# A two-layer decoder trunk on one core: gate products of two blocks in six banks, and expert stages that end by column halves and row tiles

## The chip, the cores and the metric

The kernel runs on one core of a Trainium2 chip. The core has a matrix engine (TensorE, PE in the profile; its weight loads are PEld), VectorE (DVE), ScalarE (ACT), GpSimd (POOL) and SyncE (SP, which here only issues DMAs). Products land in PSUM, eight banks of 128 partitions by 512 fp32. The metric is the device time of one execution in microseconds, the median of the runs shown.

## The reference, cut to what matters

Two layers, 512 tokens of width 1024. Layer 0 mixes tokens with a gated linear recurrence (768 channels in four blocks of 192), layer 1 with sparse attention. After each mixer comes an output projection, and after that 32 gated experts of which each token uses two.

```python
xs, gate, xq = jnp.split(hn @ w_in, [LRU_WIDTH, 2 * LRU_WIDTH], axis=-1)
xs = causal_depthwise_conv(xs, conv_w, conv_b)
# rglru: xb is xs in 4 blocks of 192 channels
r = sigmoid(einsum('bsni,nij->bsnj', xb, w_a) + b_a)
i = sigmoid(einsum('bsni,nij->bsnj', xb, w_x) + b_x)
log_a = -8 * r * softplus(-lam);  a = exp(log_a)
u = sqrt(-expm1(2 * log_a)) * (i * xf);  h = scan(a, u)
y = h * gelu(gate)
...
x = x + mixed @ w_out[i]
x = x + hier_moe(rms_norm(x, norm_ffn[i]), ...)   # (silu(xb @ w_gate[e]) * (xb @ w_up[e])) @ w_down[e]
```

## The kernel before, in words

All five engines run their own instruction stream; semaphores order them. `plan()` numbers every product group ("job") of the part outside the expert stages; job n uses PSUM bank n mod 8, and `open_bank` makes TensorE wait until the job eight numbers earlier has been read. `filled` counts finished jobs. The order of jobs is written out by hand; `lru_order()` gives it for the recurrence.

**The recurrence of layer 0.** The 768 channels are six chunks of 128, feature-major: a chunk is 128 partitions by 512 tokens. For a chunk c there are four pieces of work: `conv` (TensorE projects the chunk, eight fp32 products, each of two records; ACT copies it out at L845; DVE convolves it at L1552 and L1556), `rec` (`block_gates(c)` makes the two gate products on TensorE at L1145; ACT and DVE then run the recurrence, L856 to L866 and L1566 to L1578), and `gate` (a projection and a gelu at L873). A block has 192 channels, so three chunks hold two blocks: the weights of chunk 0 are 128 rows deep and 64 rows deep in two terms, chunk 1 is made of two column halves with two terms each, chunk 2 is chunk 0 mirrored. Before, each `block_gates(c)` makes its own chunk: 4, 8 and 4 products for the three chunks of a pair of blocks, between projections. `xc_ready` counts chunks convolved.

**An expert stage.** Each layer has 16 pairs of experts. SP streams six 2 MB weight tiles for each pair into a ring of nine buffers (`pair_weights`, L503 and L506); the first are issued when `out.0.0` of the layer is filled. For a pair TensorE makes gate and up products (L1359), transposes the hidden rows (L1365) and the next tokens (L1352), makes the down product y in two column halves of 512 (L1373; `y_psum` counts the halves), and `combine` (L1381) adds y back to the token rows through a one-hot matrix: y is split into three bf16 parts, so each of four row tiles t needs 2 x 3 products. The split goes through ACT (L1011, L1014) and DVE (L1899, L1902). DVE adds a row tile of 1024 columns to x at L1906 (`c_psum`, `c_added`). The combine of pair n is made during pair n+1. That of the last pair stands behind the loop, after the whole split, in four banks, two row tiles at a time.

**The ends.** After the last adds of a layer DVE signals `moe_done` (L1955). In layer 1 ACT waits for it before `row_norm` (L770 square, L771 root), DVE normalises the rows (L1480), TensorE transposes them (L1064) and starts the projections of layer 1 (`project_two`, L1118). After the second layer SP waits for `moe_done` and issues the four output DMAs.

Of the kernel before, what the change touches and what calls it, by code (L numbers as in the profile page):

```python
# [23 lines left out]
ALU = mybir.AluOpType  # L24
# [3 lines left out]
P = 128  # L28
D = 1024
# [222 lines left out]
def hybrid_trunk(nc, a, out):  # L252
# [8 lines left out]
    with ExitStack() as ctx:  # L261
# [3 lines left out]
        def sem(name):  # L265
            return ctx.enter_context(nc.semaphore(name))
# [93 lines left out]
        xn_ffn = area(6 * UNIT, NT, D)  # L360

# [78 lines left out]
        stored = sem("stored")  # L440
# [51 lines left out]
        BANK_HT, BANK_XT = 0, (1, 4)  # L492

# [4 lines left out]
        def _(sp):  # L498
# [22 lines left out]
            for L in range(2):  # L521
# [78 lines left out]
                if L == 0:  # L600

                    sp.wait_ge(m["y_psum"], 2 * (NP - 1))
                    w = a["dsa_w_in"][0].rearrange("(p k) n -> p k n", k=KD)
                    sp.dma_start(w_in[1][:, :, 0:C_WI], w[:, :, 0:C_WI]).then_inc(ld["win"], 16)
                    sp.dma_start(w_in[1][:, :, C_WI:], w[:, :, C_XQ:]).then_inc(ld["win"], 16)
                n_ov = sp.value_load(ov_n[0:1, 0:1], min_val=0, max_val=OVMAX)
                with sp.If(n_ov > 0):
                    sp.wait_ge(scattered, 16 * 2 * NT * (L + 1))
                    sp.wait_ge(m["y_psum"], 2 * NP * (L + 1))
                    with sp.Fori(0, n_ov) as i:  # L610
                        e = sp.value_load(ov_list[0:1, bass.ds(i * 2, 1)], min_val=0, max_val=NE - 1)
# [7 lines left out]
                        wait_alone(sp, o["y_psum"], i * 2 + 2)  # L619
            sp.wait_ge(scattered, 16 * 2 * NT * 2)  # L620
# [115 lines left out]
        def _(act):  # L736
# [64 lines left out]
            for L in range(2):  # L801
# [12 lines left out]
                row_norm(L, "mix", NT, lambda t: x[:, t, :], lambda t: xn[:, t, :], x_ready)  # L814
# [201 lines left out]
                def pair(n, first=False):  # L1016
# [4 lines left out]
                    split(m, n)  # L1021

                pair(NP * L, first=L == 0)
                with act.Fori(1, NP) as i:
                    pair(i + NP * L)
                o = ov[L]
                act.wait_ge(ld["ovl"], 16 * (L + 1))
                n_ov = act.value_load(ov_n[0:1, 0:1], min_val=0, max_val=OVMAX)
                with act.If(n_ov > 0):
                    act.wait_ge(m["c_psum"], NT * NP * (L + 1))  # L1030
                    with act.Fori(0, n_ov) as i:
                        silu_of(o, i, slice(0, CAP))
                        hidden_out(o, i)
                        split(o, i, slice(0, CAP))


        @block.tensor
        def _(pe):
# [35 lines left out]
            for L in range(2):  # L1074
# [47 lines left out]
                if L == 0:  # L1122
                    def block_gates(c):

                        if c == 0:
                            pe.wait_ge(ld["wg"], 16 * 16)
                        pair, r = c // 3, c % 3
                        for g, nm in ((0, "ra"), (1, "rx")):
                            w = gate_w[:, g, pair]
                            x0, x1, x2 = (xc[:, 3 * pair + q, :] for q in range(3))  # L1130
                            pe.wait_ge(xc_ready, 3 * pair + (2 if r == 0 else 3))
                            b = open_bank(f"0.{nm}.{c}")
                            if r == 0:
                                todo = [(slice(0, P), 0, slice(0, P))]
                            elif r == 1:
                                todo = [(slice(0, 64), 0, slice(P, LB)), (slice(64, P), 1, slice(0, 64))]
                            else:
                                todo = [(slice(0, P), 1, slice(64, LB))]
                            for part, odd, cols in todo:
                                if odd == 0:  # L1140
                                    terms = [(w[:, 0, cols], x0), (w[0:64, 1, cols], x1[0:64])]
                                else:
                                    terms = [(w[64:P, 1, cols], x1[64:P]), (w[:, 2, cols], x2)]
                                for i, (l, rr) in enumerate(terms):
                                    ins = pe.matmul(b[part, :], l, rr, start=i == 0, stop=i == 1)  # L1145
                            ins.then_inc(filled, 1)

                    for what, c in lru_order():
                        if what == "rec":
                            block_gates(c)  # L1150
# [287 lines left out]
                combine_of(n0 + NP - 1, (0, 1, 2, 3))  # L1438
# [4 lines left out]
                with pe.If(n_ov > 0):  # L1443
                    pe.wait_ge(m["c_added"], NT * (n0 + NP))
# [20 lines left out]
                pe.wait_ge(moe_done, L + 1)  # L1465
# [3 lines left out]
        def _(dve):  # L1469
# [33 lines left out]
            for L in range(2):  # L1503
# [411 lines left out]
                def pair(n, p, first=False, second=False):  # L1915
# [12 lines left out]
                    split(m, n)  # L1928
# [12 lines left out]
                dve.wait_ge(m["c_added"], NT * (n0 + NP))  # L1941
                with dve.If(n_ov > 0):
                    with dve.Fori(0, n_ov) as i:
# [11 lines left out]
                dve.memset(small[:, 252:253], 0.0).then_inc(moe_done, 1)  # L1955
# [22 lines left out]
```

## Time and profile before

| | us |
|---|---|
| median of 3 runs (1555.86 to 1560.49) | 1558.89 |
| profiled execution, its own time | 1562.51 |
| its span | 1560.6 |
| TensorE busy | 1428.0 |
| VectorE busy | 599.3 |
| ScalarE busy | 332.1 |
| mean granted TensorE clock, share of full | 0.96 |

The span is the stretch of the profiled execution from its first to its last instruction; 1.9 us of its time lie around it. Busy shares are averages over stages with different limits, so the chain of waits and the timeline have to be read stage by stage.

### The profile page before, as it was taken

What the parts mean: (1) busy time and instruction counts of PE and PEld (TensorE: products, weight loads), DVE (VectorE), ACT (ScalarE), POOL (GpSimd) and SP (SyncE); (2) the same over time, 40 slices, a digit from 0 to 9 for tenths busy, and PEclk for the clock granted to TensorE, in tenths of its full rate; (3) what the DMA queues carried; (4) which work ended last, traced back from release to release, by engine and by line L of the source; (5) the groups of instructions that cost most, each with busy time, mean ns of one, the idle gap of its engine ahead of it and who ended that gap; (6) DMA issues with size and microseconds to landing.
All of it is one profiled execution on the core that took longest, in us unless ns stands there. A gap on an engine that the chain in (4) does not pass through costs nothing.

```text
span 1560.6 us, 16585 instructions
## 1 busy us (share of the span) xinstructions
PE 1428.0 (92%) x6233; PEld 627.5 (40%) x6233; DVE 599.3 (38%) x1094; ACT 332.1 (21%) x620; POOL 103.3 (7%) x199
## 2 busy tenths in 40 slices
PE   5999889599999989999799979995999999899997
PEld 4433545433333333333364545453333333333332
DVE  2563212423343332333349965124333433322333
ACT  3266311011111110111126755110111111110110
POOL 1000100110000000000000123002000000000000
PEclk9999999599999999999999989995999999999998
DMA  8700144499999999999720020544999999999993
GB/s 314 237 0 0 54 193 198 185 379 427 425 426 427 428 427 427 430 426 428 302 92 1 21 92 1 206 171 176 406 426 427 426 428 428 427 428 426 428 428 151
DMA packets 56249, 457.36 MB, mean 293 GB/s; under 512 B 15468, under 2 KB 20124, under 8 KB 31240
## 3 DMA queue, kind: packets, MB, share of 16 engines
q1 hardware_dynamic: 49108, 447.81, 69.4%
q0 software_dynamic: 5504, 8.68, 1.5%
q8 instruction: 33, 0.54, 0.1%
q10 hardware_dynamic: 1588, 0.20, 0.1%
q14 instruction: 16, 0.13, 0.0%
HBM read 459.50 MB, written 10.53 MB: 301 GB/s over the span
## 4 chain that ended last, share of the span: by engine, by line
PE 71%; DMA 21%; DVE 3%; ACT 2%; issue 1%; ACTq 1%; POOL 0%; DVEq 0%; SPq 0%; POOLq 0%
PE ps L1055 22%; PE ps L1359 20%; DMA arena<-in_moe_w_gate 14%; PE ps L1373 10%; PE ps L1381 7%; DMA arena<-in_moe_w_up 6%; PE ps L1305 2%; PE ps L1145 2%; PE ps L1352 2%; PE ps L1064 1%; PE ps L1244 1%; PE ps L1285 1%; PE ps L1365 1%; DMA mix<-scratch_xn,idx 0%; PE ps L1342 0%
## 5 line engine op out<-in xcount | busy, mean ns | idle before, releaser
L1359 PE MATMUL ps<-arena,xT 128*64 128x512 f32 x2048 | 461.7, 604 | 33.3 <-DMA arena<-in_moe_w_gate 27.3
L1359 PEld LDWEIGHTS ps<-arena,xT 128*64 128x64 f32 x2048 | 149.0, 139 | 329.5 <-issue 325.5
L1906 DVE TENSOR_TENSOR x<-ps,x 128x1024 f32<-128x1024 f32 x128 | 156.2, 1224 | 231.7 <-PE ps L1381 229.1
L1373 PE MATMUL ps<-arena,xT 128*64 128x512 f32 x1024 | 226.8, 595 | 0.0
L1381 PE MATMUL ps<-mix,xT 128*128 128x512 bf16 x768 | 179.7, 384 | 5.7 <-ACT mix L1014 5.7
L1055 PE MATMUL ps<-xT,arena 128*128 128x512 f32 x384 | 168.7, 595 | 1.1 <-issue 1.1
L1381 PEld LDWEIGHTS ps<-mix,xT 128*128 128x128 bf16 x768 | 70.6, 99 | 134.7 <-issue 52.6
L1373 PEld LDWEIGHTS ps<-arena,xT 128*64 128x64 f32 x1024 | 70.7, 137 | 131.8 <-issue 127.9
L1055 PE MATMUL ps<-arena,mix 128*128 128x512 f32 x256 | 112.7, 600 | 3.3 <-DMA arena<-in_w_out 2.6
L1055 PEld LDWEIGHTS ps<-xT,arena 128*128 128x128 f32 x384 | 72.0, 190 | 94.2 <-issue 92.6
L1899 DVE TENSOR_TENSOR mix<-ps,mix 128x512 f32<-128x512 f32 x64 | 44.3, 691 | 169.0 <-ACT mix L1011 169.0
L1889 DVE SCALAR_TENSOR_TENSOR xT<-ps,cur,xT 128x512 f32<-128x512 f32 x32 | 24.0, 751 | 209.1 <-PE ps L1359 209.1
L1005 ACT ACTIVATE xT<-ps 128x512 f32<-128x512 f32 x32 | 19.1, 597 | 387.5 <-PE ps L1365 387.5
L1011 ACT ACTIVATE mix<-ps 128x512 bf16<-128x512 f32 x64 | 38.2, 597 | 215.4 <-PE ps L1373 215.4
L1055 PEld LDWEIGHTS ps<-arena,mix 128*128 128x128 f32 x256 | 48.7, 192 | 63.3 <-issue 60.4
L675 POOL CAST idx<-tabP 128x1 int32 (+1 forms) x34 | 6.3, 186 | 971.4 <-PE ps L1352 779.2
L1001 ACT ACTIVATE xT<-ps 128x512 f32<-128x512 f32 x32 | 19.1, 597 | 234.6 <-PE ps L1359 234.6
L668 POOL TENSOR_SCALAR arena<-arena,small 128x256 f32<-128x256 f32 (+3 forms) x80 | 39.5, 514 | 303.9 <-DVE small L1629 236.8
L1883 DVE TENSOR_TENSOR xT<-ps,gains 128x512 f32<-128x512 f32 x68 | 43.8, 686 | 13.5 <-PE ps L1352 9.2
L1352 PE MATMUL ps<-ident,mix 128*128 128x128 f32 x272 | 37.8, 284 | 11.0 <-DMA mix<-scratch_xn,idx 11.0
L1759 DVE TENSOR_TENSOR x<-ps,x 128x512 f32<-128x512 f32 x16 | 11.1, 692 | 89.0 <-PE ps L1055 89.0
L1902 DVE TENSOR_TENSOR mix<-mix 128x512 bf16<-128x512 f32 x64 | 43.9, 687 | 3.1
(230 smaller groups left out, 1131.1 us busy)
## 6 DMA issues: line engine op xcount, KB each, us to landing
arena<-in_moe_w_gate SPq DMA_DIRECT2D x64, 2048.0 KB, 29.8
arena<-in_moe_w_up SPq DMA_DIRECT2D x64, 2048.0 KB, 31.1
arena<-in_moe_w_down SPq DMA_DIRECT2D x64, 2048.0 KB, 31.8
arena<-in_lru_w_in SPq DMA_DIRECT2D x2, 3072.0 KB, 16.5
arena<-in_dsa_w_in SPq DMA_DIRECT2D x1, 5120.0 KB, 15.6
arena<-in_w_mem_kv SPq DMA_DIRECT2D x2, 2048.0 KB, 9.0
scratch_xn<-arena SPq DMA_DIRECT2D x8, 512.0 KB, 8.0
arena<-in_w_out SPq DMA_DIRECT2D x1, 4096.0 KB, 13.6
```

Source lines behind the costliest of these rows:

```text
L668: ins = pool.tensor_scalar(buf[:, h, 0:width], buf[:, h, 0:width], inv[:, h:h + 1], 1.0, ALU.mult, ALU.mult)
L1011: act.activation(y_hi[part, c, :], ps[part, BANK_Y + c, :], ACT.Copy).then_inc(q["y_high"], 1)
L1055: ins = pe.matmul(b[part, cols], l, r, start=i == 0, stop=i == len(pairs) - 1)
L1145: ins = pe.matmul(b[part, :], l, rr, start=i == 0, stop=i == 1)
L1352: ins = pe.transpose(ps[:, BANK_XT[k // 4], (k % 4) * P:(k % 4) * P + n], xg[0:n, k::KD][:, 0:P], ident[0:n, 0:n])
L1359: ins = pe.matmul(ps[e * CAP:(e + 1) * CAP, bank, :], tokT[:, k, e * CAP:(e + 1) * CAP], rows_in[u][:, k, :], start=k == 0, stop=k == KD - 1)
L1373: ins = pe.matmul(ps[e * CAP:(e + 1) * CAP, BANK_Y + c, :], hT[:, j, e * CAP:(e + 1) * CAP], rows_down[u][:, j, c * 512:(c + 1) * 512], st ...
L1381: ins = pe.matmul(ps[:, 4 + 2 * (t % 2) + c, :], onehot[part, t * P:(t + 1) * P], y[part, c, :], start=q == 0, stop=q == 2)
L1883: dve.tensor_tensor(tokT[:, 4 * q:4 * q + 4, :], ps[:, BANK_XT[q], :].rearrange("p (k n) -> p k n", k=4), gains[:, 3 * L + 2, 4 * q:4 * q ...
L1899: dve.tensor_tensor(y_rest[part, c, :], ps[part, BANK_Y + c, :], y_hi[part, c, :], ALU.subtract).then_inc(q["y_rest"], 1)
L1902: dve.tensor_tensor(y_lo[part, c, :], y_rest[part, c, :], y_mi[part, c, :], ALU.subtract).then_inc(q["y_low"], 1)
L1906: dve.tensor_tensor(x[:, t, :], ps[:, b:b + 2, :].rearrange("p a n -> p (a n)"), x[:, t, :], ALU.add).then_inc(s_, 1)
```

## The change

Four edits. (1) `lru_order()` groups the recurrence: three `conv`, three `rec`, three `conv`, two `gate`, three `rec`, four `gate`. (2) `block_gates` is called once for a pair of blocks, opens six banks, waits for three convolved chunks, and issues its 16 products sorted by their shape: whole products, then the 64-row ones (upper and lower rows in turn), then the 64-column ones, the 64 by 64 ones, and whole ones again. (3) The last pair of each expert stage leaves the loops: its split is finished one column half at a time, its combine is made by column half over all eight banks (`last_bank`), and DVE adds 128x512 pieces (`half_added` counts the left ones, `c_added` the right ones). (4) In layer 1 `row_norm` of tile t waits for the two adds of its tile alone, writes its squares to a spare area (`rows_junk`), and a Sqrt of one column is issued ahead of it; and the output DMA of tile t is issued once the two adds of its tile are there, ahead of the overflow code (no expert block overflows with these inputs; no line of that code is in the profile).

```diff
 def lru_order():
-    steps = [("conv", c) for c in range(3)]
-    for c in range(NC):
-        steps += [("rec", c), ("conv", c + 3) if c < 3 else ("gate", c - 3)]
-    return steps + [("gate", c) for c in range(NC - 3, NC)]
+    steps = [("conv", c) for c in range(3)] + [("rec", c) for c in range(3)] + [("conv", c) for c in range(3, NC)]
+    steps += [("gate", 0), ("gate", 1)] + [("rec", c) for c in range(3, NC)]
+    return steps + [("gate", c) for c in range(2, NC)]
...
+        def last_bank(t, c):
+            return (jobs.number[f"1.xT.{t}.0"] + c) % 8
...
+                else:
+                    for t in range(NT):
+                        sp.wait_ge(half_added, NT * L + t + 1)
+                        sp.wait_ge(m["c_added"], NT * (2 * NP - 1) + t + 1)
+                        sp.dma_start(out[0, t * P:(t + 1) * P, :], x[:, t, :]).then_inc(stored, 16)
...
             sp.wait_ge(moe_done, 2)
-            for t in range(NT):
-                sp.dma_start(out[0, t * P:(t + 1) * P, :], x[:, t, :]).then_inc(stored, 16)
             sp.wait_ge(stored, 16 * NT)
...
                 def x_ready(t):
-                    if t == 0:
+                    if L:
+                        act.wait_ge(half_added, NT * (L - 1) + t + 1)
+                        act.wait_ge(m["c_added"], NT * (NP * L - 1) + t + 1)
+                    elif t == 0:
                         act.wait_ge(ld["x"], 16)
                 if L:
-                    act.wait_ge(moe_done, L)
+                    act.activation(small[:, 254:255], eps[:, 0:1], ACT.Sqrt)
...
+                def split_by_half(q, n):
+                    for c in range(2):
+                        act.wait_ge(q["y_psum"], n * 2 + (1 + c))
+                        act.activation(y_hi[:, c, :], ps[:, BANK_Y + c, :], ACT.Copy).then_inc(q["y_high"], 1)
+                        act.wait_ge(q["y_rest"], n * 2 + (1 + c))
+                        act.activation(y_mi[:, c, :], y_rest[:, c, :], ACT.Copy).then_inc(q["y_mid"], 1)
...
-                    def block_gates(c):
+                    def block_gates(pair):
+                        pe.wait_ge(xc_ready, 3 * pair + 3)
+                        x0, x1, x2 = (xc[:, 3 * pair + q, :] for q in range(3))
+                        bs = [[open_bank(f"0.{nm}.{3 * pair + r}") for nm in ("ra", "rx")] for r in range(3)]
+                        for g in gates:
+                            pe.matmul(bs[0][g], w[g][:, 0, 0:P], x0, start=True, stop=False)
+                        for g in gates:
+                            pe.matmul(bs[0][g], w[g][lo, 1, 0:P], x1[lo], start=False, stop=True).then_inc(filled, 1)
+                            pe.matmul(bs[2][g], w[g][hi, 1, 64:LB], x1[hi], start=True, stop=False)
+                        for g in gates:
+                            pe.matmul(bs[1][g][lo, :], w[g][:, 0, P:LB], x0, start=True, stop=False)
+                            pe.matmul(bs[1][g][hi, :], w[g][:, 2, 0:64], x2, start=True, stop=False)
+                        for g in gates:
+                            pe.matmul(bs[1][g][lo, :], w[g][lo, 1, P:LB], x1[lo], start=False, stop=True)
+                            pe.matmul(bs[1][g][hi, :], w[g][hi, 1, 0:64], x1[hi], start=False, stop=True).then_inc(filled, 1)
+                        for g in gates:
+                            pe.matmul(bs[2][g], w[g][:, 2, 64:LB], x2, start=False, stop=True).then_inc(filled, 1)
...
-                combine_of(n0 + NP - 1, (0, 1, 2, 3))
+                last = n0 + NP - 1
+                pe.wait_ge(m["c_added"], last * NT)
+                pe.wait_ge(m["xt_sbuf"], 2 * (NP + 1) * (L + 1))
+                pe.wait_ge(m["g_done"], last + 1)
+                for c in range(2):
+                    pe.wait_ge(m["y_mid"], last * 2 + (1 + c))
+                    pe.wait_ge(m["y_low"], last * 2 + (1 + c))
+                    for t in range(NT):
+                        for q, y in enumerate(y_parts):
+                            ins = pe.matmul(ps[:, last_bank(t, c), :], onehot[:, t * P:(t + 1) * P], y[:, c, :],
+                                            start=q == 0, stop=q == 2)
+                        ins.then_inc((half_psum, m["c_psum"])[c], 1)
...
-                pe.wait_ge(moe_done, L + 1)
...
+                def last_split(n):        # DVE; rest, low: one column half of L1899, L1902
+                    dve.wait_ge(m["c_added"], n * NT)
+                    rest(0)
+                    low(0)
+                    rest(1)
+                    add(0, 0)
+                    low(1)
+                    for t in range(1, NT):
+                        add(t, 0)
+                    for t in range(NT):
+                        add(t, 1)
...
-                with dve.Fori(2, NP) as p:
+                with dve.Fori(2, NP - 1) as p:
                     pair(p + n0, p)
-                add_of(n0 + NP - 1, range(NT))
+                pair(n0 + NP - 1, NP - 1, last=True)
```

## Rows read from the trace of the kernel before

**Rows 1.** Page: busy time of the engines; the last chain by engine.

```profile
PE 1428.0 (92%) x6233; PEld 627.5 (40%) x6233; DVE 599.3 (38%) x1094; ACT 332.1 (21%) x620; POOL 103.3 (7%) x199
...
PE 71%; DMA 21%; DVE 3%; ACT 2%; issue 1%; ACTq 1%; POOL 0%; DVEq 0%; SPq 0%; POOLq 0%
```

**Rows 2.** Chain of waits in the recurrence: start us, us, what, records.

```profile
81.19 4.02 PE ps L1145 x8
...
92.27 5.03 PE ps L1145 x16
...
104.36 4.22 PE ps L1145 x8
108.58 6.87 PE ps L1055 x16
```

**Rows 3.** Timeline, weight loads of the gate products; the bracket is idle time before.

```profile
93.20 0.20 PEld L1145 LDWEIGHTS ps<-arena 64*64 64x64 f32 x4 [0.81 <-issue]
```

**Rows 4.** Timeline, cross-attention products with alternating 64-row halves.

```profile
170.23 2.00 PE L1199 MATMUL ps<-memKT,arena 64*128 64x256 f32 x16
```

**Rows 5.** Timeline of ACT, then of DVE: chunk 0's recurrence, chunk 3's convolution.

```profile
88.91 1.28 ACT L856 ACT_TABLE_LOAD   x1 [6.99 <-DVE arena L1491]
...
95.29 0.63 ACT L866 ACTIVATE arena<-arena 128x512 f32<-128x512 f32 x1
...
96.68 1.22 DVE L1578 TENSOR_TENSOR_SCAN arena<-arena 128x512 f32<-128x512 f32 x1
...
98.38 2.32 DVE L1556 SCALAR_TENSOR_TENSOR arena<-arena,prm 128x512 f32<-128x512 f32 x3
```

**Rows 6.** Chain of waits from layer 0's last down product into layer 1.

```profile
758.31 7.04 PE ps L1373 x32
...
768.19 7.04 PE ps L1381 x24
...
780.73 6.54 PE ps L1064 x32
...
789.80 7.09 PE ps L1118 x32
```

**Rows 7.** Timeline of the same boundary.

```profile
761.95 0.60 ACT L1011 ACTIVATE mix<-ps 128x512 bf16<-128x512 f32 x1 [3.89 <-PE ps L1373]
...
773.96 2.52 DVE L1906 TENSOR_TENSOR x<-ps,x 128x1024 f32<-128x1024 f32 x2 [0.49 <-PE ps L1381]
...
776.89 1.06 ACT L770 ACTIVATE mix<-x 128x1024 f32<-128x1024 f32 x1 [9.52 <-DVE small L1955]
...
778.05 1.28 ACT L771 ACT_TABLE_LOAD   x1
```

**Rows 8.** Windows: PE, PEld, DVE, ACT, POOL busy (x); granted clock; DMA; GB/s.

```profile
770.00:775.00 5.00, 5.00 (x18) 1.85 (x16) 3.17 (x3) 0.00 (x0) 0.00 (x0) 0.71 0.61 196
...
780.00:785.00 5.00, 4.27 (x20) 4.30 (x21) 3.55 (x8) 4.16 (x10) 0.00 (x0) 0.50 1.09 339
```

**Rows 9.** Page, costliest groups: an add of 128x512 from PSUM.

```profile
L1759 DVE TENSOR_TENSOR x<-ps,x 128x512 f32<-128x512 f32 x16 | 11.1, 692 | 89.0 <-PE ps L1055 89.0
```

**Rows 10.** Timeline and DMA issues: layer 1's input weights, us from issue to landing.

```profile
755.75 0.67 SPq L605 DMA_DIRECT2D arena<-in_dsa_w_in  x1
...
arena<-in_dsa_w_in SPq DMA_DIRECT2D x1, 1024.0 KB, 17.9
```

**Rows 11.** Chain of waits in the expert stages: a weight wait, the last pair's combine.

```profile
496.42 28.36 DMA arena<-in_moe_w_gate
...
1531.15 2.70 PE ps L1381 x12
...
1545.09 6.85 PE ps L1381 x24
```

**Rows 12.** Timeline: issue of the output DMAs.

```profile
1553.61 2.89 SPq L623 DMA_DIRECT2D out<-x  x4
```

**Rows 13.** Timeline of SP: first expert weights of layer 0.

```profile
217.42 0.80 SPq L503 DMA_DIRECT2D arena<-in_moe_w_gate  x2
```

More of the change, by code:

```diff
@@ L360, in hybrid_trunk @@
         xn_ffn = area(6 * UNIT, NT, D)
+        rows_junk = area(UNIT, NT, D)
         rows_in = [area(u * UNIT, KD, FE) for u in range(NU)]
@@ L439, in hybrid_trunk @@
         moe_done = sem("moe_done")
-        stored = sem("stored")
+        half_psum, half_added = sem("half_psum"), sem("half_added")
+        ov_added = [sem(f"ov_added{L}") for L in range(2)]
+        stored, restored = sem("stored"), sem("restored")
         def wait_alone(eng, s, value):
@@ L492, in hybrid_trunk @@
         BANK_HT, BANK_XT = 0, (1, 4)
+        def last_bank(t, c):
+            return (jobs.number[f"1.xT.{t}.0"] + c) % 8
+        assert sorted(last_bank(t, c) for t in range(NT) for c in range(2)) == list(range(8)) and last_bank(2, 1) == BANK_Y + 1
         block = ctx.enter_context(nc.Block())
@@ L1014, in split, with pair @@
                         act.activation(y_mi[part, c, :], y_rest[part, c, :], ACT.Copy).then_inc(q["y_mid"], 1)
-                def pair(n, first=False):
+                def split_by_half(q, n):
[4 more added lines that the diff above has]
+                        act.activation(y_mi[:, c, :], y_rest[:, c, :], ACT.Copy).then_inc(q["y_mid"], 1)
+                def pair(n, first=False, last=False):
                     silu_of(m, n)
@@ L1020, in pair @@
                         act.wait_ge(m["c_psum"], n * NT)
-                    split(m, n)
+                    (split_by_half if last else split)(m, n)
                 pair(NP * L, first=L == 0)
-                with act.Fori(1, NP) as i:
+                with act.Fori(1, NP - 1) as i:
                     pair(i + NP * L)
+                pair(NP * L + NP - 1, last=True)
                 o = ov[L]
@@ L1122, in _ @@
                 if L == 0:
-                    def block_gates(c):
-                        if c == 0:
+                    def block_gates(pair):
+                        if pair == 0:
                             pe.wait_ge(ld["wg"], 16 * 16)
[L1127 to L1146, printed above, removed]
@@ new lines, in block_gates @@
+                        pe.wait_ge(xc_ready, 3 * pair + 3)
+                        x0, x1, x2 = (xc[:, 3 * pair + q, :] for q in range(3))
+                        lo, hi = slice(0, 64), slice(64, P)
+                        gates = range(2)
+                        w = [gate_w[:, g, pair] for g in gates]
+                        bs = [[open_bank(f"0.{nm}.{3 * pair + r}") for nm in ("ra", "rx")] for r in range(3)]
+                        for g in gates:
+                            pe.matmul(bs[0][g], w[g][:, 0, 0:P], x0, start=True, stop=False)
@@ L1913, in add_of, with pair @@
                         add_tile(t, m["c_added"])
-                def pair(n, p, first=False, second=False):
+                def pair(n, p, first=False, second=False, last=False):
                     dve.tensor_copy(cur[:], tabP[:, p, :] if isinstance(p, int) else
@@ L1927, in pair, with rest, low, add @@
                     one_hot(cur[:], m["g_done"])
-                    split(m, n)
+                    if last:
+                        last_split(n)
+                    else:
+                        split(m, n)
+                def last_split(n):
+                    def rest(c):
+                        dve.wait_ge(m["y_high"], n * 2 + (1 + c))
+                        dve.tensor_tensor(y_rest[:, c, :], ps[:, BANK_Y + c, :], y_hi[:, c, :], ALU.subtract).then_inc(m["y_rest"], 1)
+                    def low(c):
+                        dve.wait_ge(m["y_mid"], n * 2 + (1 + c))
+                        dve.tensor_tensor(y_lo[:, c, :], y_rest[:, c, :], y_mi[:, c, :], ALU.subtract).then_inc(m["y_low"], 1)
+                    def add(t, c):
+                        if c == 0:
+                            dve.wait_ge(half_psum, NT * L + t + 1)
+                        else:
+                            dve.wait_ge(m["c_psum"], n * NT + t + 1)
+                        xh = x[:, t, c * 512:(c + 1) * 512]
+                        dve.tensor_tensor(xh, ps[:, last_bank(t, c), :], xh, ALU.add).then_inc((half_added, m["c_added"])[c], 1)
+                    dve.wait_ge(m["c_added"], n * NT)
[6 more added lines that the diff above has]
+                        add(t, 0)
+                    for t in range(NT):
+                        add(t, 1)
                 n0 = NP * L
@@ L1940, in _ @@
                 n_ov = dve.value_load(ov_n[0:1, 0:1], min_val=0, max_val=OVMAX)
[L1941 removed]
                 with dve.If(n_ov > 0):
+                    dve.wait_ge(half_added, NT * (L + 1))
+                    dve.wait_ge(m["c_added"], NT * (n0 + NP))
+                    if L:
+                        dve.wait_ge(stored, 16 * NT)
                     with dve.Fori(0, n_ov) as i:
@@ L1954, in _ @@
                         wait_alone(dve, o["c_added"], i * NT + NT)
-                dve.memset(small[:, 252:253], 0.0).then_inc(moe_done, 1)
+                    dve.memset(small[:, 252:253], 0.0).then_inc(ov_added[L], 1)
+                dve.memset(small[:, 253:254], 0.0).then_inc(moe_done, 1)
 _INS = ["x", "mem", "norm_mix", "norm_ffn", "mem_norm", "w_mem_kv", "xq_norm", "xk_norm", "w_out", "lru_w_in", "lru_conv_w",
```

13 lines of the change are left out of this document (11 added, 2 removed).

## The prediction, written before the changed kernel ran

> **What bounds the kernel now.** I read the page first [rows 1]: TensorE is busy 92% of the span, and the chain that ended last lies 71% on TensorE and 21% on DMA. So a TensorE microsecond counts where the chain is on it, and nothing need be gained where the chain is on a DMA. Then I took the chain in order of time, to see on which side each touched place lies. It is on TensorE without a gap all through the recurrence of layer 0 [rows 2]; it is on TensorE in the first pairs of each expert stage and on weight DMAs from 496 us on [rows 11]; and at the last pair of a stage it leaves TensorE for a relay of DVE and ACT [rows 6, 7]. The windows give the granted clock of the boundary [rows 8].
>
> Two questions decide whether time saved early is still there at the end. Does an expert stage start later work at a fixed time? Its weight stream begins at 217.42 us, right after the first output product [rows 13], so it moves with TensorE. And is layer 1's input weight in place if the boundary shrinks? It is issued at 755.75 and lands 17.9 us later, at 773.7 [rows 10]; the projections that need it begin at 789.8 [rows 6], so up to 16 us can go.
>
> **Part 1, gate products.** Before: a projection is 16 records in 6.87 us, 0.86 us a product [rows 2]. From 81.19 to 108.58 lie the gates of one pair of blocks and two projections: 27.39 - 2 x 6.87 = 13.65 us for 16 products. A change of shape costs: where each product has another shape than the last, four take 4.22 us, 1.05 each [rows 2], 0.19 more than 0.86. The middle chunk is five shape groups in 5.03 us, 1.01 each, and the 64 by 64 group holds four records of two products [rows 3]: the idle 0.81 and the 0.20 of loading show that the two products, in opposite corners of the array, together take 1.01 us, no more than one with its shape change. So side by side works for column halves with row halves.
>
> After: five groups, each of four products except the two whole ones, which hold two. A whole group costs 2 x 0.86 = 1.72. A half-size group of four costs the same 1.72 if its two halves run side by side. Four shape changes at 0.17 (between 0.15 and 0.19) are 0.7. Sum 5 x 1.72 + 0.7 = 9.3 us a pair, against 13.65: 4.35 saved, 8.7 for two pairs. The 64-row group with 512 columns is in no row; the nearest is the cross-attention's [rows 4], 16 records of 64 rows by 256 columns in 2.00 us, 0.125 each, where a record alone would take half of 0.43, 0.215. That is nearly side by side, so I take it. Bounds: if row halves run one after the other, each pair pays 1.72 more and the gain is 5.3; if shape changes cost nothing, it is 10.1.
>
> The Trainium skill's page "TensorEngine Tiling (Array Packing)", section "Key Properties", says that a change of tiling mode drains the array. The 0.15 to 0.19 us per shape change agrees with that; taken as a full stop for every one of the 16 products it would give 16 x 1.05 = 16.8 us and no gain, which the row of the 64 by 64 group contradicts, since there two products share one change.
>
> Does TensorE then wait for others? The first gate group needs three convolved chunks; DVE has convolved them while TensorE still projects and sums the query features. The second needs chunk 5 convolved, and ACT and DVE now first run recurrences 0 to 2. One takes 7.0 us on ACT (88.91 to 95.92), two table loads of 1.28 included, and the next needs nothing else from TensorE by then, since its banks are filled by 90. From 88.91, where ACT stands because of DVE's reciprocals, three end at 109.9; DVE's scan trails by 2.0 (96.68 + 1.22 against 95.92), and three convolutions of about 2.9 (97.9 to 100.7) end at 120.7 [rows 5]. TensorE gets there at 81.0 + 9.3 + 5 x 6.87 = 124.6. The cover is 3.9 us; if each recurrence took 2 us more, TensorE would wait 2.1. Recurrences 3 to 5 end about 127 + 21 = 148, and the last gate projection at 161, so four gelus are not late either. Banks: every bank that the six open is read at least 10 us before it is reopened. No cost.
>
> **Part 2, boundary to layer 1.** The left half of y is complete at 761.9, where ACT reads it [rows 7]; the relay from the end of the down product (765.35) to the combine (768.19) takes 2.84 us [rows 6]. Finished by itself the left half is ready at 761.95 + 2.84 = 764.8, before TensorE ends the right half. So 12 of 24 products start at 765.4 with no gap. At full clock 12 take 2.70 [rows 11], 768.1; the right half's relay ends at 765.35 + 2.84 = 768.2 as now; the other 12 end at 770.9. Now the 24 take 7.04 [rows 6], because the clock stood at 0.71 of full over 770 to 775 [rows 8] after that gap, and because DVE had to free banks. DVE needs 8 x 0.65 = 5.2 us in place of 4 x 1.25: 128x512 takes 0.69 alone [rows 9], 0.63 in a row, half of 2.52 / 2 [rows 7]. Its adds run from 766.7: one, then the last low part to 768.1, three left ones to 770.0, four right ones to 772.5, now 776.5.
>
> ACT can square tile 0 when add (0, 1) is done, 770.65, in place of 776.89 [rows 7]: 6.25. The table load of 1.28 that sits behind the first square [rows 7] is moved to ACT's idle time at 767.4, so the roots and all later come 6.25 + 1.28 = 7.5 earlier. Tile 3's add (772.5) is there before ACT asks for it (774.8). From the first normalised tile on the sequence is the old one: transposes (DVE normalises after its last add, 772.5, just in time), then the projections at 789.8 - 7.5 = 782.3; their weights landed at 773.7. The other loads at the start of layer 1 leave 4 us earlier. I take 7.5; low bound 5.4 if the clock falls all the same (12 products at half clock take twice 2.70, so the first right add ends near 772.8: 4.1 + 1.28).
>
> The trace has the table load at 1.28 us and the root starting right behind it. The Trainium skill's page "ScalarE: Activation LUTs", section "What ACT_TABLE_LOAD costs", gives about 2.66 with a drain; by it this term would be 8.9 in place of 7.5.
>
> **Part 3, the end.** The same relay, 776.9 us later: add (0, 1) ends at 1547.5, and SP issues the first output DMA at 1547.6 in place of 1553.61 [rows 12], so 6.0 earlier. The four issues take 2.89 and the adds come every 0.63, under the issue's 0.72, so the last issue too comes 6.0 earlier. The last store and its landing follow as now. I take 6.0; low bound 2.0: with both halves at half clock the last add ends at 765.4 + 10.8 + 0.65 = 776.9, in this stage 1553.8, where the last issue now starts at 1553.61 + 3 x 0.72 = 1555.8. The wait for `scattered` and `moe_done` is behind the stores and hidden by their flight.
>
> **Part 4, costs at nothing.** `rows_junk`, the extra semaphores, the longer code outside the loops: in the last pair DVE's and ACT's new instructions are issued under the 7 us down product; without that cover some tenths. ACT, POOL and SP lose no place in a queue that TensorE waits for.
>
> **Sum.** 8.7 + 7.5 + 6.0 = 22.2. The profiled execution's 1562.5 (1.9 around its span) would become 1540.3; it lies 3.6 above the median. From the median: 1558.9 - 22.2 = 1536.7.
>
> **Rivals.** *Gates half gained*: 64-row products run one after the other, or the second group waits for chunk 5. For it: only 3.9 us cover, and no row of this width; against it: rows 4. Price 3.4: 1540.1. *Low clock stays in the ends*: TensorE is still at half clock in the last combines. For it: it falls after gaps of 3 us [rows 8]; against: the gap in question goes. Price 2.1 + 4.0: 1542.8. *Given back in the expert stages*: weights bound them from 496 us on [rows 11], and an earlier start meets a stream no faster. Against it: the stream starts with TensorE [rows 13]. Then only the end's 6.0 is left: 1552.9. *Slower*: layer 1's projections start at half clock and stay there. The granted clock is 0.50 over 780 to 785 [rows 8], in thin transposes, and full again when the projections start. After the change the ramp is at another place, with the same gaps. Every microsecond at half clock in TensorE-bound projections costs 0.5; the change turns to a loss when it lasts more than 44 us, of about 100 us of such work. At 100 us the time would be 1536.7 + 50 = 1587. Nothing in the rows holds the clock down while TensorE is dense, so it is improbable. The Trainium skill's page "TensorE: Matmul & The Clock Gate", section "Seeing it yourself", reports a clock stuck low for 50 us; no row here shows that.
>
> **Chances and range.** Forecast 0.72, gates half gained 0.12, low clock 0.07, given back 0.04, slower 0.03, something else 0.02. A change of under 0.3% (4.7 us) can't be told from none here. All but the last three are faster by more than that, and "given back" is at its edge. Faster 0.94, same 0.03, slower 0.03. The runs shown scatter by 4.6 us, and the two bounds of part 1 reach from 1.4 better to 3.4 worse: the range is 1532 to 1544, which takes in the first two rivals.
>
> **What would show it.** Right: 32 gate records within about 9.3 us for each pair, the gate loads of 64 rows in fours; no idle TensorE ahead of the second group; the last gelu's projection ends near 161.5; a combine that starts with the down product's end; first square of layer 1 about 12 us after the down product began and the first root without a table load behind it; the output DMAs issued one after another from about 12.3 us after the start of the last down product (now 18.4). Wrong: a DVE or ACT releaser ahead of the second gate group, gate records at 0.43 spacing in the 64-row group, a half clock in the combine, or longer weight waits in the stages.

## The result, and the profile after

The changed kernel takes 1540.44 us (median of 4 runs, 1538.88 to 1541.01), the kernel before 1559.69 beside it: ratio 0.9873, 95% interval 0.9859 to 0.9888, or 19.3 us less (17.5 to 22.0). The forecast was 22.2 less, 1536.7, in a range of 1532 to 1544: the time lies in the range, and the forecast gain just above the measured interval. Measured once more beside the last experiments (c0, below) the changed kernel has 1540.38 and the ratio 0.9876 (0.9861 to 0.9891).

The two profiled spans lie 23.6 us apart, more than the medians: the profiled execution of before (1562.51) is 2.8 us above its median and that of after (1538.88) 1.6 below. So the traces are read here stage by stage, and in more than one profile. The page of the changed kernel, as in [rows 1]:

```profile
PE 1408.1 (92%) x6169; PEld 624.4 (41%) x6233; DVE 599.1 (39%) x1102; ACT 330.6 (22%) x620; POOL 103.0 (7%) x199
...
PE 70%; DMA 21%; DVE 4%; ACT 2%; issue 1%; ACTq 1%; POOL 0%; DVEq 0%; SPq 0%; POOLq 0%
```

The gate products in the chain of waits, to be read beside [rows 2]. L1165 to L1176 are the five shape groups:

```profile
81.25 1.72 PE ps L1165 x4
82.96 0.62 PE ps L1167
...
84.88 0.57 PE ps L1170
...
86.75 0.57 PE ps L1173
...
88.61 1.91 PE ps L1176 x4
90.53 34.33 PE ps L1086 x80
124.86 1.72 PE ps L1165 x4
...
134.14 27.48 PE ps L1086 x64
```

From 81.25 to 90.53 are 9.28 us for 16 products. Five projections follow, then the second group with no idle time ahead of it, then the last four projections, which begin 8.70 us earlier than before (142.84 there). The timeline of DVE shows how near the second group was to a wait: the last convolution it needs ends at 118.12 + 2.33 = 120.45, 4.4 us ahead of it.

```profile
117.55 0.54 DVE L1595 TENSOR_SCALAR arena<-arena,prm 128x512 f32<-128x512 f32 x1
118.12 2.33 DVE L1599 SCALAR_TENSOR_TENSOR arena<-arena,prm 128x512 f32<-128x512 f32 x3
```

The timeline of TensorE shows the price that no earlier row had: in the 64-row group an upper (L1167) and a lower product (L1168) start 0.01 us apart, and the pairs follow each other every 0.43 us or so.

```profile
83.43 0.59 PE L1167 MATMUL ps<-arena 64*128 64x512 f32 x1
83.44 0.59 PE L1168 MATMUL ps<-arena 64*128 64x512 f32 x1
83.86 0.59 PE L1167 MATMUL ps<-arena 64*128 64x512 f32 x1
83.86 0.59 PE L1168 MATMUL ps<-arena 64*128 64x512 f32 x1
```

The boundary to layer 1 in the timeline, beside [rows 6, 7]; the last down product starts at 748.03 in the chain (758.31 before):

```profile
755.21 2.54 PE L1478 MATMUL ps<-mix,xT 128*128 128x512 bf16 x11 [0.16 <-issue]
...
757.39 1.28 ACT L832 ACT_TABLE_LOAD   x1 [0.31 <-issue]
757.72 4.27 DVE L1992 TENSOR_TENSOR x<-ps,x 128x512 f32<-128x512 f32 x7
...
757.95 2.75 PE L1478 MATMUL ps<-mix,xT 128*128 128x512 bf16 x12 [0.20 <-DVE mix L1984]
...
760.28 1.06 ACT L787 ACTIVATE arena<-x 128x1024 f32<-128x1024 f32 x1 [1.39 <-DVE x L1992]
...
762.91 5.27 PE L1095 MATMUL ps<-ident,mix 128*128 128x128 f32 x32 [2.21 <-DVE mix L1523]
...
766.94 4.87 DVE L1539 TENSOR_TENSOR xT<-ps,gains 128x512 f32<-128x512 f32 x8
...
771.92 8.78 PE L1149 MATMUL ps<-xT,arena 128*64 128x512 f32 x32 [2.88 <-issue]
```

The combine of the left half follows the down product without a gap, both halves run at full clock, the table load stands in ACT's idle time, and the first projection starts 771.92 - 748.03 = 23.89 us after the down product in place of 31.49: 7.6 earlier. What the projection waits for is VectorE: its eight copies of the transposed rows (L1539) end at 766.94 + 4.87 = 771.81, though the profile names no releaser. But the projection takes 8.78 us where it took 7.09. The windows show why, the clock column being the one behind the five engines:

```profile
755.00:760.00 5.00, 4.64 (x23) 2.08 (x23) 4.18 (x7) 2.71 (x4) 0.00 (x0) 1.00 1.01 407
...
770.00:775.00 5.00, 3.08 (x10) 1.18 (x12) 5.00 (x5) 0.00 (x0) 0.00 (x0) 0.80 1.08 376
775.00:780.00 5.00, 5.00 (x22) 1.99 (x20) 0.83 (x2) 0.00 (x0) 0.00 (x0) 0.86 0.25 47
```

In the end stage the first output DMA is issued 12.25 us after the start of the last down product (1516.91), where it was 18.40:

```profile
1529.16 2.91 SPq L618 DMA_DIRECT2D out<-x  x4
```

But from this issue to the end of the span are 7.8 us, where they were 7.0.

### The profile page after: what moved, and what is told of

The parts are those of the page before. It is cut to its first block, busy times and chain, and to the rows that moved or that the text cites. A ratio compares the mean times of both kernels' runs of the same rounds, so it can differ in the third digit from the quotient of the medians.

```text
span 1537.0 us, 16494 instructions
## 1 busy us (share of the span) xinstructions
PE 1408.1 (92%) x6169; PEld 624.4 (41%) x6233; DVE 599.1 (39%) x1102; ACT 330.6 (22%) x620; POOL 103.0 (7%) x199
## 4 chain that ended last, share of the span: by engine, by line
PE 70%; DMA 21%; DVE 4%; ACT 2%; issue 1%; ACTq 1%; POOL 0%; DVEq 0%; SPq 0%; POOLq 0%
PE ps L1086 22%; PE ps L1390 21%; DMA arena<-in_moe_w_gate 14%; PE ps L1404 10%; DMA arena<-in_moe_w_up 6%; PE ps L1412 6%; PE ps L1336 2%; PE ps L1383 2%; PE ps L1095 1%; PE ps L1275 1%; PE ps L1316 1%; PE ps L1396 1%; PE ps L1149 1%; DMA mix<-scratch_xn,idx 0%; PE ps L1373 0%
## 5 line engine op out<-in xcount | busy, mean ns | idle before, releaser
L1390 PE MATMUL ps<-arena,xT 128*64 128x512 f32 x2048 | 462.2, 605 | 32.3 <-DMA arena<-in_moe_w_gate 25.6
L1949 DVE TENSOR_TENSOR x<-ps,x 128x1024 f32<-128x1024 f32 x120 | 146.5, 1224 | 223.2 <-PE ps L1412 220.8
L1086 PE MATMUL ps<-xT,arena 128*128 128x512 f32 x384 | 167.6, 594 | 1.1 <-issue 1.1
L1412 PE MATMUL ps<-mix,xT 128*128 128x512 bf16 x660 | 157.5, 380 | 6.4 <-issue 4.8
L1086 PE MATMUL ps<-arena,mix 128*128 128x512 f32 x256 | 112.7, 600 | 2.8 <-DMA arena<-in_w_out 2.1
L1412 PEld LDWEIGHTS ps<-mix,xT 128*128 128x128 bf16 x720 | 65.5, 98 | 119.5 <-issue 48.7
L1086 PEld LDWEIGHTS ps<-xT,arena 128*128 128x128 f32 x384 | 72.4, 190 | 93.0 <-issue 92.1
L1086 PEld LDWEIGHTS ps<-arena,mix 128*128 128x128 f32 x256 | 48.8, 192 | 62.7 <-issue 60.4
L1926 DVE TENSOR_TENSOR xT<-ps,gains 128x512 f32<-128x512 f32 x68 | 43.8, 686 | 13.5 <-PE ps L1383 9.2
```

Of the source, the lines that this page charges most:

```text
L1086: ins = pe.matmul(b[part, cols], l, r, start=i == 0, stop=i == len(pairs) - 1)
L1390: ins = pe.matmul(ps[e * CAP:(e + 1) * CAP, bank, :], tokT[:, k, e * CAP:(e + 1) * CAP], rows_in[u][:, k, :], start=k == 0, stop=k == KD - 1)
L1412: ins = pe.matmul(ps[:, 4 + 2 * (t % 2) + c, :], onehot[part, t * P:(t + 1) * P], y[part, c, :], start=q == 0, stop=q == 2)
L1926: dve.tensor_tensor(tokT[:, 4 * q:4 * q + 4, :], ps[:, BANK_XT[q], :].rearrange("p (k n) -> p k n", k=4), gains[:, 3 * L + 2, 4 * q:4 * q ...
L1949: dve.tensor_tensor(x[:, t, :], ps[:, b:b + 2, :].rearrange("p a n -> p (a n)"), x[:, t, :], ALU.add).then_inc(s_, 1)
```

## The experiments

Four marks of the chain of waits cut each profile into stretches: A, the last four gate projections start; B, the last down product of layer 0; C, the output products of layer 1; D, the last down product of layer 1; and the span's end.

| profile | A | A to B | B to C | C to D | D to end |
|---|---|---|---|---|---|
| before | 142.84 | 615.47 | 228.74 | 548.16 | 25.39 |
| after | 134.14 | 613.89 | 222.45 | 546.43 | 20.09 |
| after again (c0) | 134.18 | 615.89 | 221.97 | 547.70 | 20.16 |
| e1, gates alone | 134.11 | 614.29 | 228.46 | 546.53 | 25.71 |
| e2, ends alone | 142.92 | 615.32 | 222.38 | 546.57 | 20.11 |

A moves with the gate change, B to C and D to end with the ends, and nothing else does. A to B and C to D scatter by 2 us whatever was changed; from C to D the two profiles of the changed kernel differ by 1.3 us, and their products at L1086 alone by 1.65; what moves A to B is not shown. B to C holds such scatter too. The last long projection of layer 1 starts 128.26 us after B in the profile before, 122.35 in that after and 120.66 in c0, e7 and e9; from there to C the profiles take between 99.8 and 101.3 us, whatever the kernel. So the boundary itself gives 5.9 us where the first projection runs partly at half clock, and 7.6 where it does not.

e3, e4, e5 and e11 ran once each; they are read in their traces, and their times decide nothing.

**e1, e2: each half alone.** e1 is the kernel before with the new `lru_order` and `block_gates`; e2 is the changed kernel with both as they were.

```diff
 # e1, on the kernel before (e2 is the reverse, on the changed kernel)
-    steps = [("conv", c) for c in range(3)]
-    for c in range(NC):
-        steps += [("rec", c), ("conv", c + 3) if c < 3 else ("gate", c - 3)]
-    return steps + [("gate", c) for c in range(NC - 3, NC)]
+    steps = [("conv", c) for c in range(3)] + [("rec", c) for c in range(3)] + [("conv", c) for c in range(3, NC)]
+    steps += [("gate", 0), ("gate", 1)] + [("rec", c) for c in range(3, NC)]
+    return steps + [("gate", c) for c in range(2, NC)]
...
-                    def block_gates(c):
+                    def block_gates(pair):
```

> Only the recurrence's new order and the gate products by pairs of blocks; both stage ends as before. Theory (the steps add): the last gate projection ends 8.7 us earlier in the trace and all later work moves with it, so 8.7 us less, ratio to before about 0.9944. Rival (an earlier start is given back in the expert stages, which wait for weights): the projection ends 8.7 us earlier, but the last down product of layer 0 starts less than 4 us earlier and the ratio lies above 0.998.

> Only the stage ends; recurrence and gate products as before. Theory: boundary 7.6 us earlier up to the first projection of layer 1, of which 1.7 are lost where that projection starts at half clock, and 5.3 at the end: 11.2 us less, ratio about 0.993. Rival (the profile of the changed kernel was a lucky one, the forecast terms hold in full): 13.5 us less, ratio 0.9914. Rival (the ends hardly matter, the gates carry the gain): under 6 us, ratio above 0.996.

e1: ratio 0.9934 (0.9920 to 0.9947), 10.3 us less by it and 9.3 by the medians (1550.76 against 1560.09). e2: 0.9932 (0.9919 to 0.9946), 10.6 less. B starts 9.9 us earlier in e1 than in the profile of before, so nothing of it is given back to the weight stream. The two add to 20.9 by the ratios, beside 19.3 for both together (17.5 to 22.0): the halves add. e2's interval is 8.4 to 12.6 us less: the 11.2 of its theory lie in it, and both its rivals, 13.5 and under 6, outside.

**e3: is taking turns needed for row halves to run side by side?**

```diff
                         for g in gates:
                             pe.matmul(bs[0][g], w[g][lo, 1, 0:P], x1[lo], ...)
+                        for g in gates:
                             pe.matmul(bs[2][g], w[g][hi, 1, 64:LB], x1[hi], ...)
```

> The changed kernel with one edit: in the 64-row group both upper products are issued first, then both lower ones, in place of turns. Theory (two 64-row products run side by side only when they stand next to each other in the order): two of the four run alone, so the group of four takes about 0.43 to 0.86 us more in each pair of blocks, 9.3 becomes 9.7 to 10.2 us. Rival (the order inside a group of one shape does not matter, the array runs as soon as a half is free): 9.3 us stays.

My theory fell. From 81.11 to 90.39 are 9.28 us, as before the edit. The timeline of e3 shows an upper product (L1167) and a lower one (L1169) start together, though both upper ones stand first in the program:

```profile
82.75 0.69 PE L1167 MATMUL ps<-arena 64*128 64x512 f32 x1
82.77 0.69 PE L1169 MATMUL ps<-arena 64*128 64x512 f32 x1
```

**e4: how much cover has the second gate group?**

```diff
-    steps += [("gate", 0), ("gate", 1)] + [("rec", c) for c in range(3, NC)]
+    steps += [("gate", 0)] + [("rec", c) for c in range(3, NC)]
```

> The changed kernel with the projection of gate 1 moved behind the second group of gate products, so that one projection of 6.87 us less stands ahead of it. Theory (the recurrences of ACT and DVE set when the second group can start, 120.5 us): TensorE arrives at 118.0 and waits 2.5 us, with DVE as the releaser, and the last gate projection ends 2.5 us later than in the changed kernel, 164.1. Rival (the cover is larger than the timeline says, or the wait is absorbed later): no wait, 161.6.

The wait is there, 2.50 us with DVE as the releaser. But the last projection ends 5.2 us later than in the changed kernel, not 2.5: 0.7 of it had arisen before 81 us, and the rest, 1.9, is work at half clock behind the wait. The timeline of e4 has 3.07 us for the first four records behind the wait; the changed kernel has 1.88 for them in the same view.

```profile
118.85 2.33 DVE L1599 SCALAR_TENSOR_TENSOR arena<-arena,prm 128x512 f32<-128x512 f32 x3
...
121.24 3.07 PE L1165 MATMUL ps<-arena 128*128 128x512 f32 x4 [2.50 <-DVE arena L1599]
124.24 1.22 PE L1167 MATMUL ps<-arena 64*128 64x512 f32 x1
```

**e5: the Sqrt ahead of the row norms** is left out.

```diff
-                if L:
-                    act.activation(small[:, 254:255], eps[:, 0:1], ACT.Sqrt)
-                else:
+                if not L:
```

> The changed kernel without the one-column Sqrt ahead of the row norms of layer 1. Theory (the table load is the whole price): the load of 1.28 us stands again behind the first square, and the first transposes of layer 1 start 1.3 us later after the start of the last down product than in the changed kernel (14.9 there). Rival (the Trainium skill's figure with a drain): 2.7 us later.

```profile
760.17 1.06 ACT L787 ACTIVATE arena<-x 128x1024 f32<-128x1024 f32 x1 [3.20 <-DVE x L1989]
...
761.34 1.28 ACT L788 ACT_TABLE_LOAD   x1
...
763.97 5.65 PE L1092 MATMUL ps<-ident,mix 128*128 128x128 f32 x32 [3.38 <-DVE mix L1520]
...
773.09 7.09 PE L1146 MATMUL ps<-xT,arena 128*64 128x512 f32 x32 [2.61 <-issue]
```

The load is back, the root comes 1.28 us later and the first transposes 1.2 (16.05 us after the down product at 747.92, in place of 14.88). The Trainium skill's page "ScalarE: Activation LUTs", section "What ACT_TABLE_LOAD costs", adds a drain, for 2.66 us in all; no such second part shows here: the root starts at 762.63, right behind the load. And the first projection, 1.3 us later in its start, ran at full clock, so it ended 0.4 us earlier than in the profile after (32.3 against 32.7 us after the down product). Against c0, where it starts at 23.9 and runs at full clock too, it ended 1.3 us later.

**e11: the first row norm waits for all adds.**

```diff
-                        act.wait_ge(half_added, NT * (L - 1) + t + 1)
-                        act.wait_ge(m["c_added"], NT * (NP * L - 1) + t + 1)
+                        act.wait_ge(half_added, NT * L)
+                        act.wait_ge(m["c_added"], NT * NP * L)
```

> The changed kernel, but the first row norm of layer 1 waits for all eight adds instead of the two of its tile. Theory: its first square starts 13.9 us after the start of the last down product in place of 12.25, so everything up to the first projection comes 1.6 to 1.8 us later, 25.6 in place of 23.9. Rival (DVE is the limit there anyway, since it normalises only after its last add): less than 0.5 us later.

The start of the first projection moves as the theory says, to 774.32 - 748.64 = 25.7 us after the down product, 1.8 later. Its end hardly moves against the profile after, 32.8 against 32.7, again for the clock (31.0 in c0):

```profile
762.68 1.06 ACT L787 ACTIVATE arena<-x 128x1024 f32<-128x1024 f32 x1 [3.19 <-issue]
...
774.32 7.09 PE L1149 MATMUL ps<-xT,arena 128*64 128x512 f32 x32 [2.52 <-issue]
```

**e7: work in the wait before that projection.**

```diff
+                def fill(b, n):
+                    for i in range(n):
+                        pe.matmul(b, ident[:], iota_tok[:], start=True, stop=True)
                 norm_sum(f"{L}.memK")
+                if L:
+                    wait_emptied(pe, "1.xT.0.1")
+                    fill(bank("1.kk"), 3)
```

> The changed kernel with three fp32 products of constants (128x128 by 512, 0.86 us each at full clock) put on TensorE between the sum of the memory keys' squares and the first projection of layer 1, into the bank that this projection overwrites; nothing of the result is touched. Theory (the 2.9 us of idle time there let the clock fall): the projection takes 7.1 us in place of 8.78 and all later work comes 1.7 us earlier, unless the fillers themselves run at half clock, when they end 2.3 us late. Rival (the low level comes from the thin transposes before it, not from the idle time): the projection still takes 8.8 us.

```profile
770.91 2.74 PE L1140 MATMUL ps<-iota_tok,ident 128*128 128x512 f32 x6
774.01 7.09 PE L1156 MATMUL ps<-xT,arena 128*64 128x512 f32 x32 [0.36 <-issue]
```

Same start after the down product (23.9), full clock, 1.7 us less, and B to C is 221.21. In the time it can't be told from the changed kernel: 0.9871 (0.9856 to 0.9886). The low clock is also not certain to come: five profiles with the changed boundary and no fillers have 8.78 us there (after, e2, e3, e4, e6), two have 7.09 (e9, c0) at the same start. The waits ahead of it differ: 2.88 to 2.94 us in the five, 2.61 in the two, whose transposes took 0.3 us longer. The transposes of e7 ended as early as in the five, and its projection ran at full clock; this speaks against the rival and for the wait.

**e9 and e6: the longer tail of the stores.** e9 issues the four stores behind the last add.

```diff
+                    sp.wait_ge(half_added, NT * L + NT)
+                    sp.wait_ge(m["c_added"], NT * 2 * NP)
                     for t in range(NT):
-                        sp.wait_ge(half_added, NT * L + t + 1)
-                        sp.wait_ge(m["c_added"], NT * (2 * NP - 1) + t + 1)
                         sp.dma_start(out[0, t * P:(t + 1) * P, :], x[:, t, :])
```

> The changed kernel with all four output DMAs issued behind the last add instead of each behind its own two. Theory (the stretch from the last store's issue to the end of the span, 4.9 us against 4.1 before the change, is longer because the first stores start while DVE still adds and so run unevenly): the first issue comes 1.7 us later, but issue to end is 7.0 us again as before the change, so the end comes 0.9 us later. Rival (the longer tail has nothing to do with the per-tile waits): issue to end stays 7.8 and the end comes 1.7 us later.

The first issue comes 14.05 us after the down product (1517.65), 1.8 later, and from it to the end are 7.2 us; D to end is 21.25. So the tail is shorter by 0.6 to 0.7 when the stores stand together, and issuing them early is still worth 1.1 us, in one profile of e9. The ratio, 0.9882 (0.9867 to 0.9897), agrees and can't resolve it.

```profile
1531.70 2.95 SPq L618 DMA_DIRECT2D out<-x  x4
```

e6 tried a cause: SP's overflow branch stands behind the stores, and its jump might fetch instructions while they are in flight.

```diff
-                n_ov = sp.value_load(...)
-                with sp.If(n_ov > 0):
+                if L == 0:
+                    n_ov = sp.value_load(...)
+                    with sp.If(n_ov > 0):
```

> The changed kernel without the overflow branch of SP in layer 1 (left out: SP's part in overflow blocks, of which these inputs have none). Theory (the branch behind the four stores makes SP fetch instructions by DMA while the stores are in flight, and one DMA engine finishes late): the stretch from the start of the last down product to the end of the span falls from 20.1 us to about 19.3, and no stray store packets follow the bulk. Rival (the landing of stores that are issued while the adds still run is slower for another reason): 20.1 stays.

D to end stays 20.14 (ratio 0.9870, 0.9849 to 0.9892). That theory fell, and why stores issued during the adds finish late stays open.

**e8, e10: work in the waits before dense stretches.** e8 is e7 with fillers at three more places; e10 adds more.

```diff
+                    if L == 0 and m_ == 0:          # x_turn(0)
+                        first = open_bank(...); fill(first, 5)
...
+                b = open_bank(f"{L}.rank"); fill(b, 3)       # e10 only
+                b = open_bank(f"{L}.table"); fill(b, 2)      # e10: 3
                 pe.wait_ge(placed, L + 1)
...
+                fill(ps[:, 7, :], 4)                         # before the first token transposes
                 pe.wait_ge(gathered, 16 * ((NP + 1) * L + 1))
...
+                        if t == 2: fill(b, 2)                # e10 only, third router product
```

> The changed kernel with such fillers in these waits of TensorE: three as in the kernel before this one, five before the first transposes of layer 0's cross-attention, and in each layer two before the table products and four before the first token transposes of the expert stage. Theory (each wait of more than about 3 us is followed by work at half clock, and fillers prevent it): 1.7 us at the first projection, about 1.5 at the cross-attention, 1.0 + 1.8 at the start of the expert stage of layer 0 and 1.0 + 2.8 in layer 1: up to 9 us less than the changed kernel, ratio to before about 0.982. Rival (fillers run at half clock and delay what follows as much as they save): no faster than the changed kernel, 0.987.

> The kernel with fillers in four waits, and in each layer two more ahead of the third router product, three ahead of the rank products and three in place of two ahead of the table products. Theory: the third and fourth router products and the transposes between them run at full clock (3.5 us less in each layer), and the table products of layer 1 too (1.7): about 6 to 8 us less than the kernel with four, ratio to before about 0.978. Rival (fillers that run at half clock are late by as much as they save): ratio 0.982 or more.

e8: 1533.81 us, ratio 0.9821 (0.9807 to 0.9834), the ratio of its theory. e10: 1526.74 us, ratio 0.9790 (0.9776 to 0.9803), which overlaps neither e8's interval nor the changed kernel's. It lies 7.1 us under e8 by the medians, as its theory has it, but the parts are not all as named there: in layer 0 the fourth router product ends 2.1 us earlier than in the changed kernel (270.65 in place of 272.77), not 3.5. The start of layer 0's expert stage, first in the changed kernel (its 64 records take 15.81 in the chain), then in e10:

```profile
282.12 3.65 PE L1373 MATMUL ps<-xT 128*128 128x64 f32 x16 [4.17 <-DVE xT L1883]
291.27 1.95 PE L1383 MATMUL ps<-ident,mix 128*128 128x128 f32 x8 [5.49 <-DMA mix<-scratch_xn,idx]
```

```profile
279.93 2.02 PE L1389 MATMUL ps<-xT 128*128 128x64 f32 x16 [1.42 <-DVE xT L1894]
282.92 6.50 PE L1140 MATMUL ps<-iota_tok,ident 128*128 128x512 f32 x8 [0.97 <-DVE tabP L1913]
289.25 1.04 PE L1399 MATMUL ps<-ident,mix 128*128 128x128 f32 x8
291.84 13.96 PE L1406 MATMUL ps<-arena,xT 128*64 128x512 f32 x64 [1.54 <-DVE xT L1943]
```

Table products 3.65 to 2.02, transposes 1.95 to 1.04, gate and up products 15.8 to 14.0. Four fillers took 6.50 us there, so they ran at half clock for a part, and the transposes follow them with no wait for the tokens any more: they still paid. A to B and C to D fall to 609.7 and 541.0 us.

**c0: the changed kernel again.**

> The changed kernel unchanged, on the same chip as the three others, to compare them with. Expected: ratio to before 0.987 within its interval.

It gave 0.9876, and in its profile the projection at 23.9 us takes 7.09.

## Why the prediction was right, step by step

The time alone would not have told: 1540.44 lies as near to the rival "gates half gained" (1540.1) as can be. It is the trace that excludes that rival, since A moved by the whole 8.7.

**Gates, 8.7.** Right in sum and parts: 9.28 us a pair for the 9.3 of the sum, from the row of the 64 by 64 group; A moved by 8.70. That 64-row halves run side by side, the one price that no row had, is shown by the pairs in the timeline and by e3. One sign of being wrong was badly worded: records of the 64-row group do stand 0.43 us apart, but two at a time. The cover was 4.4 us for the 3.9 of the working (TensorE came at 124.86, DVE ended at 120.45), and e4, with one projection less in it, turned it into a wait of 2.50. e1 alone gives 9.3 to 10.3 us; what it has beyond 8.7 is inside its interval (8.3 to 12.5).

**Boundary, 7.5.** Right up to the start of the first projection (7.6 for 7.5); the last add ends 14.0 us after the down product for the forecast's 14.2. The step that was mis-sized is the sentence that "from the first normalised tile on the sequence is the old one". The instructions were, the clock was not: the transposes ran faster (5.27 us for 6.54), but VectorE's copies behind them did not (4.87 us both times), so TensorE waited 2.9 us instead of 1.7, and the projection began partly at half clock. That takes back 1.7 us in five profiles, where the boundary gives 5.9, and nothing in c0, e9 and e7, where it gives 7.6. e5 and e11 show the same from the other side: 1.3 and 1.8 us less of head start left the end of that projection where the profile after has it, within 0.4 us. The rival "low clock stays in the ends" had the mechanism but the wrong place; the combines ran at full clock.

**End, 6.0.** The issue came 6.15 us earlier, and 5.3 are left at the end of the span (5.6 against e1). The step that was off: "the last store and its landing follow as now". They take 0.8 to 0.9 us longer. e9 shows that most of that hangs on starting the stores during the adds; by what mechanism is open.

**Sum.** 8.7 + 5.9 + 5.3 = 19.9 from the rows with the half clock in that projection, 21.6 without it, for 22.2 forecast, and the ratio gives 19.3 (17.5 to 22.0). "Given back in the expert stages" is excluded by e1, whose last down product starts 9.9 us earlier; "slower" came nowhere near: the half clock in that projection lasted about 3.4 us, twice the 1.7 lost.

## What to carry to other kernels

An order in which all products of one array shape stand together, with complementary row or column halves in the same group, can be priced from a single row that shows two halves in one slot; and before a producer is moved, add up the chain of the other engines that feeds its second use, because the cover is a number (here 4 us) and what is over it costs more than its length. When a wait of TensorE is shortened, look at what becomes of the next one: a head start that only lengthens the following wait may be paid back in clock. A few useless products in such a wait can prevent that: at the first projection they gave 1.7 us in the profile and nothing that the time can show (e7), and in all the waits of e10 together 13.7 us below the changed kernel by the medians, more than the head start of the boundary.

## What the runs showed of the hardware

- Two 64-row products into different banks start within 0.02 us of each other even when the other product of the upper half stands between them in the program (e3).
- A wait of 2.50 us in a dense stretch cost 4.4 us: TensorE's granted clock was 0.70 in the stretch that holds its end and the work behind it (e4): its lower level, 1.2 GHz, for a part, and 2.4 GHz for the rest. The Trainium skill's page "TensorE: Matmul & The Clock Gate", section "HAM oscillation — how this bites in real kernels", has the same effect for waits on DMA; here waits on DVE do it, of 2.50 us in e4 and of 2.88 to 2.94 ahead of the first projection (8.78 us behind them). The length alone does not decide: behind waits of 2.52 to 2.61 at that place the projection took 7.09 (c0, e5, e9, e11).
- Stores that start while VectorE still adds into the same tensor take 7.8 to 7.9 us from first issue to the end, and 6.9 to 7.2 together behind the last add (6.9 in e1, 7.0 before, 7.2 in e9).

```profile
120.00:125.00 5.00, 3.76 (x6) 1.33 (x8) 1.15 (x2) 0.00 (x0) 0.00 (x0) 0.70 0.00 0
```

The window is e4's, 120 to 125 us, the wait's last part included.
